# First expert block of a mixture-of-experts layer: its rows selected on TensorE by one-hot products in place of an indirect DMA

## What is computed

```python
def hier_moe(h, w_rg, b_rg, w_re, b_re, w_gate, w_up, w_down):
    ...
    grp_prob = jax.nn.softmax((hf @ w_rg).astype(jnp.float32) + b_rg.astype(jnp.float32), axis=-1)
    p_grp, g_idx = lax.top_k(grp_prob, 1)
    ...
    w_top, e_loc = lax.top_k(jax.nn.softmax(sel_logits, axis=-1), TOP_K)
    w_top = p_grp * w_top / jnp.sum(w_top, axis=-1, keepdims=True)
    ...
    for e in range(N_EXPERTS):
        a = jax.nn.silu(hf @ w_gate[e]) * (hf @ w_up[e])
        y = y + gates[:, e:e + 1] * (a @ w_down[e])
    return y.reshape(B, L, D)
```

## Time and profile before

| | us |
|---|---|
| median of 3 runs | 804.22 |
| lowest and highest of them | 802.68, 804.98 |
| the profiled execution's own time | 803.55 |
| its span in the profile | 801.7 |
| PE busy | 760.3 (95%) |
| DVE busy | 605.2 (75%) |
| ACT busy | 458.9 (57%) |
| POOL busy | 73.6 (9%) |

### The profile page before, as it was taken

The page is one execution under the profiler, slowest core; times in us unless marked ns, Lnnn a source line. Parts: engine busy times, 40 slices in busy tenths (PEclk is TensorE's granted clock), DMA queues, the critical chain, the costliest instruction groups (busy, mean ns, idle before and its releaser), DMA issues.

```text
span 801.7 us, 11083 instructions
## 1 busy us (share of the span) xinstructions
PE 760.3 (95%) x3804; PEld 620.6 (77%) x3804; DVE 605.2 (75%) x929; ACT 458.9 (57%) x676; POOL 73.6 (9%) x86
## 2 busy tenths in 40 slices
PE   5899999999999899989897998999999999999994
PEld 3665868788898799978785696888888888888883
DVE  5767483996889778833447468799998999999882
ACT  5942333121243867622359342688877888888773
POOL 0000000000000000000000001112222232322111
PEclk8999999999999999999999998899999999999998
DMA  8730303020130110012221376899999999999841
GB/s 291 290 105 1 91 15 105 27 79 1 53 88 19 48 59 2 2 52 79 79 79 53 139 277 258 336 396 373 360 373 378 376 393 372 376 373 379 337 176 21
DMA packets 28543, 146.54 MB, mean 183 GB/s; under 512 B 4791, under 2 KB 6711, under 8 KB 21976
## 3 DMA queue, kind: packets, MB, share of 16 engines
q1 hardware_dynamic: 23320, 135.53, 44.8%
q0 software_dynamic: 5184, 10.50, 5.0%
HBM read 141.81 MB, written 12.58 MB: 193 GB/s over the span
## 4 chain that ended last, share of the span: by engine, by line
PE 76%; DVE 9%; ACT 7%; DMA 4%; issue 2%; SPq 0%; POOL 0%; ACTq 0%; POOLq 0%; DVEq 0%
PE bank L1912 17%; PE bank L1850 16%; PE bank L2278 10%; PE bank L2280 10%; PE bank L2279 10%; PE bank L1857 3%; PE bank L2273 2%; DMA slot<-in_w_down 2%; PE bank L1924 1%; ACT pr L938 1%; PE bank L2192 1%; PE bank L2190 1%; PE bank L2191 1%; PE bank L2315 1%; DVE w_lo L1108 1%
## 5 line engine op out<-in xcount | busy, mean ns | idle before, releaser
L1769 DVE TENSOR_TENSOR e_lo<-slot,e_hi 128x1024 fp32r<-128x1024 f32 x192 | 221.3, 1218 | 7.7 <-ACT e_hi L988 7.6
L988 ACT ACTIVATE e_hi<-slot 128x1024 fp32r<-128x1024 f32 x192 | 188.0, 1061 | 5.4 <-DMA slot<-in_w_down 3.7
L1108 DVE TENSOR_TENSOR w_lo<-w_raw,w_hi 128x1024 fp32r<-128x1024 f32 x41 | 49.4, 1222 | 75.6 <-ACT w_hi L694 75.5
L694 ACT ACTIVATE w_hi<-w_raw 128x1024 fp32r<-128x1024 f32 x41 | 42.6, 1057 | 101.2 <-DMA w_raw<-in_w_in 63.4
L2278 PE MATMUL bank<-e_hi,hgT_hi 128*128 128x512 f32 x240 | 94.9, 395 | 0.0
L2280 PE MATMUL bank<-e_hi,hgT_lo 128*128 128x512 f32 x240 | 93.6, 390 | 0.0
L2279 PE MATMUL bank<-e_lo,hgT_hi 128*128 128x512 f32 x240 | 93.4, 389 | 0.0
L2280 PEld LDWEIGHTS bank<-e_hi,hgT_lo 128*128 128x128 f32 x240 | 45.1, 188 | 9.6
L2278 PEld LDWEIGHTS bank<-e_hi,hgT_hi 128*128 128x128 f32 x240 | 45.3, 189 | 8.9
L2279 PEld LDWEIGHTS bank<-e_lo,hgT_hi 128*128 128x128 f32 x240 | 45.1, 188 | 8.9
L2278 PE MATMUL bank<-e_hi,gaT_hi 128*128 128x512 f32 x120 | 48.1, 401 | 0.0
(11 more groups left out here) (392 smaller groups left out, 1710.0 us busy)
## 6 DMA issues: line engine op xcount, KB each, us to landing
slot<-in_w_down SPq DMA_DIRECT2D x16, 2048.0 KB, 15.6
slot<-in_w_gate SPq DMA_DIRECT2D x16, 2048.0 KB, 14.7
slot<-in_w_up SPq DMA_DIRECT2D x16, 2048.0 KB, 14.8
w_raw<-in_w_in SPq DMA_DIRECT2D x18, 512.0 KB, 3.6
w_raw<-in_w_out SPq DMA_DIRECT2D x8, 512.0 KB, 3.7
w_raw<-in_w_k_mem SPq DMA_DIRECT2D x4, 512.0 KB, 6.3
x_in<-in_x SPq DMA_DIRECT2D x4, 512.0 KB, 9.3
w_raw<-in_w_v_mem SPq DMA_DIRECT2D x4, 512.0 KB, 5.3
```

The lines of the kernel that those rows point to most:

```text
L694: act.activation(w_hi[ring(m)][:], w_raw[ring(m)][:], ACT.Copy).then_inc(s_wh, 1)
L988: act.activation(e_hi[buffer(b, j)][:], slot[slot_][:, 1024 * part:1024 * (part + 1)], ACT.Copy).then_inc(s_ehi, 1)
L1108: dve.tensor_tensor(w_lo[slot_][:], w_raw[slot_][:], w_hi[slot_][:].bitcast(F32), ALU.subtract)\
L1769: dve.tensor_tensor(e_lo[slot_][:, at_], slot[slot_][:, at_], e_hi[buffer(b, j)][:].bitcast(F32), ALU.subtract)\
```

## The change

Block 0's rows no longer come through DRAM. DVE makes `first_oh`, for each token the one-hot of its row in block 0 (a row of zeros if it isn't there), from the smaller of its two numbers `blocks * 128 + places`. PE multiplies `xn`, in plain float32, with `first_oh`: eight chunks of 128 features, each summed over four tiles of 128 tokens, 32 products of 128 columns, whose results stand transposed in banks 0 and 1 as the transposes left them. The first half (16 products) stands ahead of the product `records`, the second behind it. The gather of block 0, its transposes and the fillers behind `records` go; `gates` is made inside block 0, ahead of its third piece. `xn` lies elsewhere in memory, and `count` and `records` take banks 5 and 6, so that banks 0 and 1 are free.

```diff
-        xn = at("xn", 136, [P, TT, D])
+        xn = at("xn", 152, [P, TT, D])
...
+        first_oh = at("first_oh", 136, [P, TT, P])
...
-            elif j[0] == "gates":
+            elif j[0] in ("count", "records", "gates"):
                 number[j] = len(number)
-                b = 7
+                b = {"count": 5, "records": 6, "gates": 7}[j[0]]
...
             wait_freed(sp_, ("router", TT - 1))
-            for q in range(2):
-                sp_.wait_ge(s_gath[q], 16)
+            sp_.wait_ge(s_gath[1], 16)
...
-            gather(0, 0)
             gather(1, 1)
             wait_freed(pool, ("gates",))
...
             inc = R(880, 16)
+            near = R(2856, 4)
+            link(dve.scalar_tensor_tensor(R(2864, 8), blocks, float(P), places, ALU.mult, ALU.add))
+            link(dve.tensor_tensor(near, R(2864, 4), R(2868, 4), ALU.min))
+            dve.tensor_tensor(first_oh[:], iota[:].unsqueeze(1).to_broadcast([P, TT, P]), near.unsqueeze(2).to_broadcast([P, TT, P]),
+                              ALU.is_equal).then_inc(s_foh, 1)
             block_oh = rt[:, 1880:2072].rearrange("p (g b) -> p g b", b=MAXB)
...
+            def first_rows(half):
+                for k in range(4):
+                    c = 4 * half + k
+                    for t in range(TT):
+                        ins = pe.matmul(banks[half][:, k * P:(k + 1) * P], xn[:, t, c:D:KT], first_oh[:, t, :], start=(t == 0), stop=(t == TT - 1))
+                ins.then_inc(s_t, 1)
+
+            for b in range(2):
+                pe.wait_ge(freed[b], uses[b])
             job = ("records",)
             open_bank(pe, job)
             keep_clock(bank(job)[:], 20)
+            pe.wait_ge(s_foh, 1)
+            pe.wait_ge(s_xn, 2 * TT + 2)
+            first_rows(0)
             for g in range(2 * TT):
                 if g % TT == 0:
                     pe.wait_ge(s_slot, g // TT + 1)
                 ins = pe.matmul(bank(job)[:, 0:MAXB], place_oh[:, g, :], rhs_i[:, g, :], start=(g == 0), stop=(g == 2 * TT - 1))
             done(ins)
-            job = ("gates",)
-            open_bank(pe, job)
-            keep_clock(bank(job)[:], 5)
-            pe.wait_ge(s_grhs, 1)
-            done(accumulate(job, bank(job)[:, 0:2 * MAXB],
-                            [(place_oh[:, g, :], rhs_g[:, g].rearrange("p c b -> p (c b)")) for g in range(2 * TT)]))
-
+            first_rows(1)
+
+            def gates_job():
+                job = ("gates",)
+                open_bank(pe, job)
+                pe.wait_ge(s_grhs, 1)
+                done(accumulate(job, bank(job)[:, 0:2 * MAXB],
+                                [(place_oh[:, g, :], rhs_g[:, g].rearrange("p c b -> p (c b)")) for g in range(2 * TT)]))
 
             for b in range(7):
                 pe.wait_ge(freed[b], uses[b])
-            keep_clock(banks[6][:], 8)
...
                 for j in range(8):
+                    if first and j == 2:
+                        gates_job()
                     if first and j == 4:
                         rows_T(1, 1)
...
-            rows_T(0, 0)
-            keep_clock(banks[6][:], 3)
             turn(0, 0)
```

More of the change, by code:

```diff
@@ L360, in build @@
         s_slot = sem("slot_onehots_ready")
+        s_foh = sem("first_block_onehots_ready")
         s_wr = sem("router_weights_split")
@@ L630, in _ @@
             for q in range(2):
-                pool.wait_ge(s_gath[q], nb * 8)
+                pool.wait_ge(s_gath[q], nb * 8 - 16 * (1 - q))
         @block.scalar
@@ L2253, in _ @@
             done(ins)
-            job = ("gates",)
-            open_bank(pe, job)
-            keep_clock(bank(job)[:], 5)
-            pe.wait_ge(s_grhs, 1)
-            done(accumulate(job, bank(job)[:, 0:2 * MAXB],
-                            [(place_oh[:, g, :], rhs_g[:, g].rearrange("p c b -> p (c b)")) for g in range(2 * TT)]))
+            first_rows(1)
[5 more added lines that the diff above has]
+                                [(place_oh[:, g, :], rhs_g[:, g].rearrange("p c b -> p (c b)")) for g in range(2 * TT)]))
             for b in range(7):
                 pe.wait_ge(freed[b], uses[b])
-            keep_clock(banks[6][:], 8)
             def rows_T(b, q):
-                pe.wait_ge(s_gath[q], (b - q) * 8 + 16)
+                pe.wait_ge(s_gath[q], (b - q) * 8 + 16 * q)
                 if not isinstance(b, int) or b >= 1:
```

## The result

The changed kernel takes **811.69 us** (median of 9 runs) beside 804.98 for the kernel before in the same session (9 runs): ratio 1.0079, interval 1.0056 to 1.0102, so 0.8% slower. By the ratio that is 6.4 us, with 4.5 to 8.2 by its interval; the medians differ by 6.7. The forecast was 807.7, at most 810.0. Its sign was right and its size was not. The execution that was profiled took 813.02 us, its span is 811.2.

What follows compares the result with a forecast made beforehand. The prediction took PE to bound the kernel from block 1 on. It summed 803.55 (the profiled execution) + 2.0 (block 1 starting late) + 2.2 (low clock) = 807.7 us, range 804.3 to 810.0.

Steps and rivals of the forecast that it cites:

- Step 1: On DVE ahead of `place_oh`: three new instructions, `first_oh` 0.64 us of them, make everything behind 1.06 us later.
- Step 2: On PE, the first 16 new products: 0.223 us each, from 495.42 to 498.99; the other bound was 0.11 each.
- Step 3: `records` behind the first half takes about 1.15 us; `rec_i`, for which DVE waits, starts 3.1 us late.
- Step 4: DVE's pieces and `hgT_lo` follow `rec_i`; PE starts block 0 at 507.5, 1.0 us late.
- Step 5: The second 16 products run under DVE's pieces, free; removed fillers and transposes win nothing; PE idles from 503.4 to 507.5.
- Step 6: `gates` inside block 0 costs PE 0.9 us and DVE's slack of 1.57; block 1 starts 2.0 us late in all.
- Step 7: Gather 1 issued about 3.1 us later, SP's loads of block 1 about 1 us later; all taken as nothing.
- The premise that what happens ahead of block 1 counts one for one: From block 1 on PE sets the pace, so the end moves with block 1's start on PE, 518.65 before.
- The clock: PE idle 4 us ahead of block 0 means a low clock at block 0's start: plus 2.2 us, bounds 0 and 3.0.
- A: Rival: the clock stays up over PE's gap ahead of block 0, giving 805.6 us; chance 0.15.
- B: Rival: new products cost half, block 0 starts one us earlier, 803.6 us at full clock or 805.7 at low; chance 0.1.
- D: Rival: DVE loses its slack again in block 1, or weight loads collide, adding 2 to 3 us: 810; chance 0.1.

Runs made afterwards that it cites:

- e1: The changed kernel with `xn` stored by chunks, so that the new products' stationary operand is contiguous; ratio 1.0056 against the kernel before.
- e7: e1 with added groups of 16 products or transposes that nobody reads, at several operand strides, ahead of block 0; one profiled run, 868.6 us.
- e1b: The kernel of e1 run a second time, unchanged; ratio 1.0046 against the kernel before.
- e3: The changed kernel with `records` moved ahead of the first half of the new products, stride as it was; ratio 1.0067 against the kernel before.
- e6: The kernel before with only `gates` moved inside block 0, its rows still gathered; ratio 0.9995 against the kernel before.
- e9: The kernel before with 10 fillers in place of 5 ahead of `gates`; ratio 1.0006 against the kernel before.
- e4: The changed kernel with `gates` taken out of block 0 to right behind the second half of the new products; ratio 1.0059 against the kernel before.
- e8: e1 with 16 fillers in PE's gap ahead of block 0; ratio 1.0062 against the kernel before.
- e8b: The kernel of e8 run a second time, unchanged; ratio 1.0029 against the kernel before.
- e2: The changed kernel with the edits of e1 and e3 together; ratio 1.0017 against the kernel before.

## Why the prediction was right and wrong

**Step 1, DVE's three instructions: right.** `first_oh` ends at 495.79 (495.09 + 0.70), forecast 495.32; it takes 0.70 us, forecast 0.64 by half of `place_oh`. The two small ones cost 0.2 us each, as forecast; that it is 0.47 late is the wait for `count`, 0.7 us, less 0.27 by which this execution reached `onehots` earlier.

**Step 2, the price of the new product: wrong, and this is the step that failed.** I took 0.22 us each from the earlier trace rows, bounded by 0.11 from the earlier trace rows. Measured: 7.91 / 16 = 0.49 and 7.71 / 16 = 0.48. I matched the rows by type and number of columns, and not by how the operand lies in memory: the operand of the earlier trace rows lies side by side, that of the new product at every eighth float. The only strided operand in my rows was that of the transposes, where the stride does not show in the price (0.88 us for eight with it, 0.87 without), so that both ends of my bound were on the cheap side. e1 and e7 show the cause by taking it away and by measuring it alone.

**Step 3, `records` behind the first half: right in its mechanism,** wrong by the term of step 2. With the cheap product `rec_i` is 3.2 us late (e1b, 11.9 for 8.7), forecast 3.1; in the changed kernel it is 7.9, of which the dearer products are 4.3 and the wait for `count` 0.7.

**Step 4, DVE decides, and PE idles 4 us: wrong for the changed kernel, right for e1b.** From `rec_i` to the pieces it is 1.97 us, as forecast, and `hgT_lo` follows them directly. But with 15.6 us of products PE is done with the second half at 512.25, hardly later than DVE with `hgT_lo` (511.84), and e3 shows that PE holds block 0 even with DVE out of the way. In e1b PE is idle from 504.5 to 508.4, and block 0 is 1.1 us late, forecast 1.0.

**Step 5, the second half is free: wrong,** by step 2. Its 7.7 us no longer fit under DVE's 6.5 us from `rec_i` to `hgT_lo`. The other half of this step, that the fillers it removes had cost nothing, was a wrong reading of the rows as well: e6 and e9 show that they held the transposes in the kernel before.

**Step 6, `gates` in block 0 costs 1.0 us between block 0 and block 1: right,** 1.2 by e4 (13.2 for 12.0), and DVE's 1.57 us went as forecast. I had not counted what the move wins ahead of block 0, 0.8 us, which the changed kernel gets because PE is the bound there.

**Step 7, DMA at nothing: right,** with a larger slip than forecast. The gather is issued 7.7 us later, SP's first load of block 1 5.5 later (510.15 for 504.68), and no wait in front of block 1's `e_hi` shows. The 10 to 12 us that I gave each load were a guess: in the kernel before the two took 7.6 and 13.4.

**The premise that what happens ahead of block 1 counts one for one: roughly so for losses, not for e9's gain.** The stages of the changed kernel, e4 and e1b are 7.0, 6.5 and 4.7 us longer, their ratios stand for 6.4, 4.8 and 3.7 us. e9's lead of 2.2 us gave nothing in the time.

**The clock: the term is real, and the changed kernel doesn't have it.** Its 2.2 us were tied to the idle gap, and the dear products filled the gap. Four stretches of the changed kernel:

```profile
497.00:498.00 1.00, 1.00 (x6) 1.00 (x6) 0.90 (x4) 0.00 (x0) 0.00 (x0) 1.00 0.00 0
...
499.00:500.00 1.00, 1.00 (x6) 1.00 (x6) 0.00 (x0) 0.00 (x0) 0.00 (x0) 0.50 0.00 0
...
502.00:503.00 1.00, 1.00 (x6) 1.00 (x6) 0.00 (x0) 0.00 (x0) 0.00 (x0) 1.00 0.00 0
...
512.00:513.00 1.00, 1.00 (x6) 0.84 (x6) 0.08 (x1) 0.71 (x2) 0.00 (x0) 1.00 0.65 213
```

Block 0 starts at full clock. Where the gap exists (e1b), the low clock costs 2.6 us at block 1, and 3.5 in e1 against e8; the forecast had 2.2, with bounds of 0 and 3.0. This is read from the stage, and the kernels' times don't confirm it. The Trainium skill (TensorE: Matmul & The Clock Gate, HAM oscillation) says that a wait between bursts of products throttles PE and that the next burst starts cold: e1b agrees, with PEclk at 0.50 from 507, inside an idle gap of 3.88 us that ends at 508.4, until 513.

**The sum.** 803.55 + 2.0 + 2.2 was a loss of 4.2 us. The changed kernel's stage is 7.0 longer, 6.3 without the wait for `count`, where steps 1 to 6 had 2.0; the medians differ by 6.7. With the one term mended (e1b) the stage is 4.7 longer, and the ratio of 1.0046 is 3.7 us. The 807.7 was also counted from one execution that lies 1.4 us below the median of 804.98; from that median the same loss gives 809.2.

**The rivals.** A (clock stays up) came out right about the clock and wrong about the cause. It is e8b that is A: stage 2.0 us longer, to the tenth what A said, and 1.0029. B (products at the price of a transpose) was on the wrong side of the earlier trace rows; I should have asked for a row that is dearer than the earlier trace rows as well as for one that is cheaper. C (faster, DVE's order doesn't hold) fell. D (2 to 3 us more, so a loss of 6.2 to 7.2) had the right size, for causes that did not happen: that is luck. It was the same with "wrong if the clock stays full": in block 0 it did, and the forecast was wrong, but the sign that mattered was the first in the list, 32 records in 3.6 us.

## What to carry to other kernels

Before you price a product by a row of the trace, match the row in four things: type, columns, role of each operand, and its step in memory. In the probe a step of four or eight floats doubled every narrow product but the transposes; a tile that a transpose reads with a stride for nothing can be a dear operand of a product, and the layout is cheaper to mend at the producer (0.2 to 0.7 us here, against 8.5 us of products). Fillers are work like any other, and at half clock nearly twice as long: count how long those ahead of a reader take at the clock they will get, and compare that with when its data land. Here eight of them took 3.76 us and held the rows, and five more, put where PE waited, brought the eight down to 2.07.

## What the hardware showed that I had not expected

- A narrow plain float32 product with the stationary operand at every fourth or eighth float takes 0.47 us in place of 0.22, and 0.45 with the moving operand at every eighth; with fp32r and a stationary operand at every eighth it is 0.24 in place of 0.12. At every second float it is 0.24. The transpose keeps its price of 0.11, though its weight load goes from 140 to 188 ns. With 512 columns a product takes 0.84.
- The strided products take the same time at half clock: in the stretches of the changed kernel above, six records run in the us from 499 at PEclk 0.50, and six in those from 497 and 502 at 1.00. Those with the floats side by side do not: in e2 six records run in the us from 501 at 0.50, and eleven in the one from 505 at 1.00.
- The granted clock was at half from 498 to 501 and again from 505 to 508, in stretches where PE is shown busy for the whole of each us, with those same products. Ahead of the fall at 498 PE had been idle for 0.88 us, up to 495.83, and then at them for two us without a pause. Why the clock fell is not shown here.
- The gathered rows of 128 places landed about 4.2 us after the issue of the gather (498.17 to 502.4 in e6, 498.31 to 502.4 in e9), while the fillers in front of their transposes ran until 504.17 in the kernel before.
